# A recurrence over 64-token chunks: keys and values on the opposite half of the partitions, and the next tile's keys made between the small and the whole blocks

## The reference

```python
def wkv_step(S, inp):
    r_t, w_t, k_t, v_t, kk_t, a_t = inp
    sa = jnp.einsum('bhvk,bhk->bhv', S, -kk_t)
    S = (S * w_t[:, :, None, :] + sa[..., None] * (kk_t * a_t)[:, :, None, :]
         + v_t[..., None] * k_t[:, :, None, :])
    y = jnp.einsum('bhvk,bhk->bhv', S, r_t)
    return S, y
```

## Time and profile before

| what | us |
|---|---|
| median of 3 executions | 1159.81 |
| lowest and highest | 1158.47, 1163.6 |
| the profiled execution, whole time | 1162.31 |
| its span | 1160.5 |
| TensorE, busy in the span | 1101.3 (95%) |
| VectorE, busy | 665.4 (57%) |
| ScalarE, busy | 365.8 (32%) |
| GpSimd, busy | 214.0 (18%) |

### The profile page before, as it was taken

One profiled execution on the slowest core, in us unless ns is written; L12 is line 12 of the kernel. 1 busy time (PEld: TensorE's weight loads), 2 busy tenths in 40 slices (PEclk: granted clock), 3 DMA queues, 4 the chain that ended last, 5 costly groups with the idle time before them and its releaser, 6 DMA issues.

```text
span 1160.5 us, 24234 instructions
## 1 busy us (share of the span) xinstructions
PE 1101.3 (95%) x9392; PEld 666.0 (57%) x9393; DVE 665.4 (57%) x1154; ACT 365.8 (32%) x720; POOL 214.0 (18%) x278
## 2 busy tenths in 40 slices
PE   7999999999998799999989999967999999999986
PEld 5666666666666688999984555534333333333342
DVE  6288999993554687888744232365343343433416
ACT  6000011011322657777641211022223232232324
POOL 4000000010001113332320001001233233333200
PEclk9999999999998899999999999977999999999999
DMA  9211111010000111111233321057998889999739
GB/s 270 79 36 37 37 37 37 27 43 23 1 1 8 19 20 24 23 20 22 54 136 99 105 73 51 31 225 285 380 348 330 301 329 342 419 406 403 317 125 389
DMA packets 97791, 171.45 MB, mean 148 GB/s; under 512 B 44490, under 2 KB 69249, under 8 KB 88419
## 3 DMA queue, kind: packets, MB, share of 16 engines
q1 hardware_dynamic: 90211, 152.31, 36.8%
q0 software_dynamic: 7488, 17.84, 4.4%
HBM read 153.64 MB, written 25.91 MB: 155 GB/s over the span
## 4 chain that ended last, share of the span: by engine, by line
PE 82%; DMA 6%; DVE 5%; SPq 3%; ACT 2%; issue 1%; POOLq 0%; DVEq 0%; ACTq 0%
PE ps L1655 27%; PE ps L2120 14%; PE ps L1970 10%; PE ps L2150 8%; PE ps L1667 7%; PE ps L1688 3%; PE ps L2107 2%; DMA arena<-y_rows 2%; PE ps L1676 1%; PE ps L2000 1%; DMA arena<-in_w_exp_down_dram 1%; SPq L537 1%; PE ps L2136 1%; DMA late<-in_w_gate_up_dram 1%; PE ps L1985 1%
## 5 line engine op out<-in xcount | busy, mean ns | idle before, releaser
L1655 PE MATMUL ps<-arena 128*128 128x384 f32 (+1 forms) x1032 | 316.6, 468 | 0.0
L1655 PEld LDWEIGHTS ps<-arena 128*128 128x128 f32 x1032 | 195.3, 190 | 118.0 <-issue 1.9
L2120 PE MATMUL ps<-arena 128*64 x416 | 188.5, 596 | 4.1 <-DVE arena L2860 1.7
L2123 PE MATMUL ps<-arena 128*64 128x512 f32 x416 | 188.5, 596 | 0.0
L2272 DVE SCALAR_TENSOR_TENSOR arena<-arena,cw 128x1024 f32<-128x1024 f32 x240 | 168.2, 778 | 0.4
L2120 PEld LDWEIGHTS ps<-arena 128*64 128x64 f32 x416 | 54.5, 136 | 112.6 <-issue 112.5
L1970 PE MATMUL ps<-arena 128*128 128x512 f32 x256 | 113.1, 596 | 0.0
L1667 PE MATMUL ps<-arena 64*64 64x64 f32 x2960 | 97.5, 219 | 5.0 <-DVE arena L2606 1.6
L2150 PE MATMUL ps<-arena 128*64 x208 | 96.5, 607 | 2.4 <-ACT arena L1412 2.4
L2153 PE MATMUL ps<-arena 128*64 128x512 f32 x208 | 96.5, 607 | 0.0
L1667 PEld LDWEIGHTS ps<-arena 64*64 64x64 f32 x2960 | 92.0, 135 | 7.2 <-issue 4.8
(11 more groups left out here) (368 smaller groups left out, 1527.5 us busy)
## 6 DMA issues: line engine op xcount, KB each, us to landing
arena<-in_w_exp_gate_dram SPq DMA_DIRECT2D x32, 1024.0 KB
arena<-in_w_exp_up_dram SPq DMA_DIRECT2D x32, 1024.0 KB
arena<-in_w_exp_down_dram SPq DMA_DIRECT2D x32, 1024.0 KB, 10.4
arena<-in_w_in_dram SPq DMA_DIRECT2D x22, 512.0 KB, 4.0
arena<-in_x_prompt_dram SPq DMA_DIRECT2D x16, 512.0 KB, 7.8
arena<-y_rows SPq DMA_DIRECT2D x8, 1024.0 KB, 17.0
arena<-in_w_out_dram SPq DMA_DIRECT2D x2, 2048.0 KB
xn_rows<-arena SPq DMA_DIRECT2D x8, 512.0 KB, 2.8
```

Of the source, the lines that this page charges most:

```text
L1655: ins = pe.matmul(banks(proj_bank(q) + piece)[:, 0:n1 - n0], win[q % 6][:, c, :], xnT[:, c, n0:n1], start=(c == 0), stop=(c == DC - 1))
L2120: pe.matmul(banks(b)[0:HS, :], xgT[b][:, c, 0:HS], wring_gu[:, bass.ds(slot, 1), 0:2, c, :].rearrange("p a w f -> p (a w) f"), start=(c == ...
L2123: ins = pe.matmul(banks(b)[HS:P, :], xgT[b][:, c, HS:P], wgu[b][:, :, c, :], start=(c == 0), stop=(c == DC - 1))
```

## The change

- Opposite halves. Values and keys in token order are written to the other half (values and keys of the head on partitions 0 to 63 go to 64 to 127), and so is the k gram. The products with them read one half and write the other, and are issued in turn with products that stay on their half: value tokens with the b gram, key tokens with b tokens, the k gram with level 4's products, the key part of the right side with level_y 4, the key part of the state with level_y 5 or with chain_u of chunk 1, the key part of the output with chain_u or with the state part. The last turn of the prompt keeps the sampled tile's grams and tokens on their own half.
- PSUM banks. The chain's right side, solution and state alternate between banks 7 and 6; the b tokens go to bank 6 from tile 1 on, and the keys' bank is 1 from tile 2 on.
- The order of the turn on VectorE and ScalarE, as below.
- The convolution group's norm, tanh and swish are done for 512 tokens at a time around the last projections and in the first turn, and for the 64 sampled tokens after the last turn.

SyncE's `invert_blocks` is unchanged. The diff, cut to its core:

```diff
+            def product(hp, dst, lhs, rhs, first=True, last=True, alone=False, half=same):
+                for p in (0, 64):
+                    h, k = slice(p, p + 64), half(p)
+                    ins = pe.matmul(dst[h, hp * 64:hp * 64 + 64], lhs[k, hp, :], rhs[k, hp, :],
+                                    start=alone or (first and hp == 0), stop=alone or last, skip_group_check=True)
+                return ins
...
+            def gram_and_values(j):
+                for c in range(2):
+                    if j >= 2:
+                        pe.wait_ge(y_done, 2 * j - 3 + c)
+                    for hp in range(CT):
+                        first_gram = gram_of(hp, j, c, bt, same)
+                        value = token(hp, c, 0, values(j), other)
+                first_gram.then_inc(gb_psum, 1)
+                value.then_inc(tok_psum, 1)
...
+            def turn(j):
+                i = j - 1
+                n = 2 * i
+                scaled_ready(j)
+                gram_and_values(j)
...
+                decay(j + 1, decay_bank(j + 1))
+                iclr(j + 1)
...
+                for c in range(2):
+                    x = level_in(i, 4, c)
+                    for hp in range(CT):
+                        if c == 0:
+                            rhs_keys(i, 0, hp)
+                        ins = product(hp, banks(4 + c)[:, 0:256], PT[i % 2][:, c, :, :], x, alone=True)
+                    ins.then_inc(yl_psum, 1)
...
+                for c in range(2):
+                    pe.wait_ge(mm_done, level_count(i, 4, c))
+                    m, xt = MM[:, c, :, :], XX[:, 1, c, :, :]
+                    for hp in range(CT):
+                        product(hp, banks(4 + c)[:, 0:256], xt, m, alone=True)
+                        key_gram = gram_of(hp, j, c, kt, other)
+                        ins = product(hp, banks(4 + c)[:, 256:512], m, xt, alone=True)
+                    ins.then_inc(xx_psum, 1)
...
+                key_tokens(j)
...
+                first_u(i)
+                if j >= 3:
+                    to_channels(j - 3, 4)
+                else:
+                    bonus(i)
+                first_state(i)
+                if j >= 3:
+                    bonus(i)
+                second_rhs(i)
+                cumulate(j + 1)
+                second_u(i)
+                if j >= 3:
+                    gate(j - 3, 4)
+                second_state(i)
```

ScalarE's turn afterwards:

```diff
+            def turn(j):
+                i = j - 1
+                if j >= 3:
+                    gn_root(j - 3)
...
+                x_copies(i, 5)
+                u_copy(2 * i)
                 if j >= 3:
+                    gn_affine(j - 3, 4)
+                rhs_copy(2 * i + 1)
+                y_copy(i, 0, 2)
+                exps(j + 1)
+                key_scale(j + 1)
+                u_copy(2 * i + 1)
+                blocks_turned(j)
                 if j >= 2:
                     gn_square(j - 2)
+                y_copy(i, 1, 3)
```

VectorE's turn, and the convolution group's norm:

```diff
+            def turn(j):
                 first_level(j, mask_ar)
+                first_gb(j, mask_ar)
+                level_masks(j - 1, 4)
                 decay_add(j + 1)
                 if j >= 2:
                     gn_centre(j - 2)
                 if j >= 3:
                     gn_inverse(j - 3)
-                if j:
-                    conv_norm(j - 1, 0)
-                    conv_norm(j - 1, 1)
                 masked_k(j, mask_ar)
+                level_masks(j - 1, 5)
                 small_blocks(j)
+                keys(j + 1)
+                new_state(j - 1, 0)
                 whole_blocks(j)
-                keys(j + 1)
+                bonus_v(j - 1)
                 scaled_a_b(j + 1)
+                new_state(j - 1, 1)
...
+            def conv_norm(p):
+                dve.wait_ge(cstd_done, p + 1)
+                link(dve.reciprocal(conv_std(p), conv_std(p)))
+                v = conv_rows(p)
+                dve.tensor_tensor(v, v, conv_std(p).unsqueeze(1).broadcast_to(v.shape), ALU.mult).then_inc(ln_step, 1)
...
             conv(len(taps))
             link(dve.tensor_tensor(eye2, ident[:, 0:64], ident[:, 64:128], ALU.add))
-            dve.memset(x_flat, 0.0)
             scaled_a_b(0)
+            conv_norm(1)
+            conv_swish(0)
```

More of the change, by code:

```diff
@@ L1259, in powers_copy, with first_turn @@
                 ins.then_inc(s8_in, 1)
-            for j in range(NT):
+            def first_turn():
+                decay_tanh(1)
+                tok_copy(0, 0, vtok, 0)
+                iclr_tanh(1)
+                tok_copy(0, 1, btok, tok_bank(0))
+                norms_wide(1)
+                tok_copy(0, 2, ktok, 0)
+                exps(1)
+                blocks_turned(0)
+                key_scale(1)
+                act.wait_ge(zs_done, ZT)
+                act.activation(zs[:, GL0, :], zs[:, GL0, :], ACT.Tanh, scale=0.5).then_inc(gl_tanh, 1)
+            def turn(j):
                 i = j - 1
@@ L1276, in _ @@
[L1276 to L1281, removed]
-                tok_copy(j, 2, ktok, 0)
[L1283 to L1287, removed]
-                if j >= 3:
[L1289 to L1295, removed]
-                    blocks_turned(0)
@@ L1324, in _ @@
+            first_turn()
+            for j in range(1, NT - 1):
+                turn(j)
+            last_turn_of_prompt()
+            conv_tanh(2)
             gn_root(NT - 3)
@@ L1660, in _, with same, other @@
                 between(q - NCONV)
-            def heads(dst, lhs, rhs, first=True, last=True, alone=False):
+            def same(p):
+                return slice(p, p + 64)
+            def other(p):
+                return slice(64 - p, P - p)
+            def product(hp, dst, lhs, rhs, first=True, last=True, alone=False, half=same):
[4 more added lines that the diff above has]
+                return ins
@@ L1664, in heads @@
+            def heads(dst, lhs, rhs, first=True, last=True, alone=False, half=same):
                 for hp in range(CT):
-                    for p in (0, 64):
-                        h = slice(p, p + 64)
-                        ins = pe.matmul(dst[h, hp * 64:hp * 64 + 64], lhs[h, hp, :], rhs[h, hp, :],
-                                        start=alone or (first and hp == 0), stop=alone or last, skip_group_check=True)
-                return ins
-            def to_tokens(j, b, src):
+                    ins = product(hp, dst, lhs, rhs, first, last, alone, half)
+                return ins
@@ L1678, in to_tokens, with gram_of, values @@
                 ins.then_inc(tok_psum, 1)
-            def gram(j, lhs, done):
+            def gram_of(hp, j, c, lhs, half):
+                t = slice(c * 64, c * 64 + 64)
+                for p in (0, 64):
+                    h = slice(p, p + 64)
+                    ins = pe.matmul(banks(2 + c)[half(p), hp * P:(hp + 1) * P], lhs[h, hp, t],
+                                    AR[j % 3][h, hp, :, t], start=True, stop=True)
+                return ins
+            def values(j):
+                return zs[:, V0:V0 + CT, j * P:j * P + tokens_of(j)]
@@ L1681, in gram @@
+            def gram(j, lhs, done, half=same):
                 for c in range(chunks_of(j)):
@@ L1895, in _ @@
+                first_state(i)
+                sample_inverse(3)
+                state_in(1)
+                second_rhs(i)
+                state_in(2)
+                second_u(i)
+                gate(j - 3, 4)
+                state_in(3)
+                second_state(i)
+            first_turn()
+            for j in range(1, NT - 1):
+                turn(j)
+            last_turn_of_prompt()
             pe.wait_ge(s_sum, 2 * (NT - 1))
```

531 lines of the change are left out of this document (292 added, 239 removed).

## The result

The changed kernel takes 1184.2 us (median of 4 runs, 1179.97 to 1186.62). Run beside it, the kernel before took 1161.7. The ratio is 1.0194, with a 95% interval of 1.0165 to 1.0224: **slower by 1.9%**. The profiled execution took 1179.97 us, the fastest of the four, with a span of 1178.2 us (before: 1160.5). The trace therefore explains 17.7 us of the median's 22.5.

A forecast was written before the change was run, and what follows sets the result against it. TensorE and SyncE's round trip were both near limits; the change makes SyncE's loop the bound. Six turns +21.6, last turn +4.9, TensorE behind it -0.5: +26.0 us, 1185 on the median's footing; range 1170 to 1208.

The forecast's parts named there:

- SyncE's closed loop: In-order block transfers, tile to tile: 23.1 us with 2.6 slack before, 28.3 after and then the bound.
- first DMA issue to small blocks, low clock included: SyncE's first block issue to VectorE's small blocks: 9.7 us hop plus 1.0 for TensorE's low clock.
- from there to the next L604: Hop back through SyncE, from the end of blocks_turned to the next tile's first block issue: 7.3 us.
- last turn, to the inverse: Last prompt turn, until level_y gets tile 7's inverse: 31.1 us instead of 26.2, +4.9.
- first turn: Conv norm pieces in VectorE's idle time before first_level(0): taken as 0 us, bounds -0.5 and +1.5.
- marks: Trace signs listed to confirm or refute the forecast: turn spacing, SyncE's waits, blocks_turned's place, TensorE's idle and clock, packing times.
- The engine part: Strict chain from the blocks' arrival to the end of blocks_turned: 11.3 us, where it was 6.0.
- The low clock: TensorE at 1.2 GHz after idling before level_y, delaying small blocks: 1.0 us a turn, bounds 0 and 2.
- The packing: Opposite-half products overlapping their partners on TensorE: 6.4 us less work a turn, bounds 0 and 6.45.
- no overlap: Rival: opposite-half pairs on TensorE do not overlap at all; turns 33.6 us, total 1215; chance 0.08.
- Little packing: Rival: TensorE keeps one record in 29 ns, only grams hide some; turns 32.3 us, total 1206; chance 0.10.
- Faster: Rival: SyncE's loop does not decide, turns fall to the engines' need, 22.3 us; total 1137; chance 0.05.

The follow-up runs named there:

- e1: Kernel before the change, with only blocks_turned of tiles 1 to 7 moved behind u_copy of the second chunk on ScalarE; 1185.65 us, ratio 1.0227.
- e9: Changed kernel with 24 float32 filling products on TensorE ahead of its wait for the inverse; 1193.85 us, ratio 1.0263.
- e4: Changed kernel with keys and values back on their own half, same issue order; 1210.56 us, ratio 1.0403.
- e8: Changed kernel with VectorE's whole_blocks before keys and new_state, gated and gn_variance behind first_level, cumulate before second_rhs, ScalarE's blocks_turned first, key_scale last; 1184.71 us.
- e10: e8 with 12 float32 filling products on TensorE ahead of its wait for the new tile's keys; 1168.04 us, ratio 1.0041.
- e13: e10 with the gate's 8 products ahead of cumulate, replacing 5 of the 12 filling products; 1163.77 us, ratio 1.0020.
- e12: e8 with VectorE's keys before whole_blocks, ScalarE's exps before blocks_turned, 8 filling products before cumulate and gate between cumulate and second_rhs; 1179.98 us, ratio 1.0166.

## Why the prediction was right

The forecast was 1185.0 us and slower; measured were 1184.2 and slower. The mechanism, SyncE's closed loop, stands. That the numbers meet within 1 us is in part luck, since the terms do not meet that well. The parts of a turn are means of the six:

| term | forecast us | measured us |
|---|---|---|
| first DMA issue to small blocks, low clock included | 9.7 + 1.0 | 9.86 |
| small blocks to end of blocks_turned | 11.3 | 11.57 |
| from there to the next L604 | 7.3 | 6.88 |
| a turn | 29.3 | 28.31 |
| six turns against before | +21.6 | +15.7 |
| last turn, to the inverse | +4.9 | +3.4 |
| first turn | 0 | -1.9 |

**SyncE's loop: right.** e1 shows it without the rest of the change: blocks_turned behind the exps makes L587 follow L601 at once and gives 28.68 us a turn. Two marks came out: L604 no longer waits for first_level, and blocks_turned follows u_copy directly. So did the idle stretch of over 4 us ahead of level_y (4.7 to 5.6 in five of the six turns, 0.2 in the first). The clock near 0.8 did not: 0.86 to 0.95.

**The engine part: 0.3 short on average, and for two reasons.** The first two turns took 11.0 us, a little under the forecast. The four from 443.92 on took 11.7 to 12.0. In all four the bonus products hold TensorE for 0.2 to 0.7 us after new_state is done; the prediction had new_state release the second right side. And in two of them (472.63 and 502.38) the second half of new_state (L2677) lasted 1.08 and 1.05 us instead of 0.42, beside a GpSimd addition (L898) that had begun 0.5 and 0.7 us earlier. In the other two that addition began only as L2677 ended, and the next operation on VectorE, L2661, took 1.22 and 1.24 us instead of 0.18. The pattern holds in four turns; it was not tried by itself.

**The low clock: the term that was wrong.** The prediction let the half clock after the idle wait push the small blocks back by 1.0 us, to 10.7 us behind L604. They start 9.86 behind it on average, which leaves this term 0.2 us and not 1.0, if the hop is the 9.7 of the forecast. The half clock came, with 0.86 to 0.95 on average where about 0.8 was expected. The failed step is the end of level_masks 5, put at 10.8 us behind L604. It was at 9.0 us in the turn from 502.38, 1.07 before the blocks arrived, and at 9.5 and 10.3 in the two turns where the DMA did not release the small blocks. e9 with 1.00 for 0.91 gained nothing. What is left open is whether the low clock has a share in the 0.2 to 0.7 us by which TensorE is late for the second right side.

**The packing: right, with one number of it wrong.** e4 against the changed kernel: TensorE's busy time is 26.44 and 20.91 us a turn, means of six, 5.5 less; forecast was 6.4. Both have stretches at half clock, so this is not the work alone. In the list of marks I gave 0.95 us for the value tokens with the b gram. They take 1.9 (524.82 to 526.7), the gram's own time, which is what the working above it implied. The rule of the Trainium skill (TensorE: Matmul & The Clock Gate, the section that asks why 56 ns and not 53.3), by which matmuls start no closer than about 25 ns, would have limited this. The 61 records at 14.5 ns each do not agree with it, and the measurement decides: with four corners at work it does not bind here. The prediction's "rows and columns each overlap alone" went further than its rows: the pairs of L1667 differ in both.

**The rivals.** e4 has no product on the opposite half and so stands for "no overlap", which was put at 1215; it took 1210.56. "Little packing" (1206) did not happen and has no run of its own. "Faster" stood on blocks_turned ending within 6 us of the blocks' arrival. e8 met that (small blocks from 514.09, blocks_turned from 519.44 to 520.09) and was not faster: the prediction did not see the second loop, which keeps the mean turn above 26 us in every order that ran. So its condition for that rival does not give that rival's figure, 1137. No packed kernel's median came under that of the kernel before.

**The sum** came out better than its terms, and that is luck. On the profiled execution's footing it was +26.0 in the span, and 17.7 were measured. The medians rose by 22.5: the profiled execution of the changed kernel was 4.2 us under its median, and the kernel before ran at 1161.7 beside it and not at the 1159.8 that the forecast started from. The first turn's -1.9 is partly scatter: with the same first turn, the second L604 fell anywhere from 389.93 to 391.17 in the packed kernels. What sets the remaining turns of e10 and e13, 24.4 to 28.6 us each, stays open but for one thing: L604 starts 0.02 to 0.03 us after first_level in every one of them.

## What to carry to other kernels

Where a queue serves two ends of a round trip in order, write the trip down as a loop (issue, hop, engine part, hop back) and compare it with the period before anything is moved. An instruction of 0.65 us that only feeds a DMA must keep its place when its queue is rearranged; e1 lost 24.6 us by it. Work saved on an engine is time only if the loops that don't pass it are shorter, and a wait put into that engine's own chain can cost twice, once as the wait and once as the half clock behind it. Filling products help there, if they end before the wait does (e10), and hurt where they don't (the first of e9's turns, e12).

## What was not expected of the hardware

Four corners of the array together took one 64-column record in 14.5 ns, twice the rate of two. A low clock left no visible cost in one order (0.91 over three turns) and cost about 3 to 4 us a turn in another (0.83 over two), with the same work. SyncE's eight issues of L604 took 3.71 us in some turns and 5.06 in others, and one issue of them up to 1.78 us where the rest took 0.43. That did not set the turn's first part by itself: the small blocks came 11.08 us after the first issue with 3.72 us of issues, and 8.77 with 4.37.
